# Summing the fourth channel chunk of a 31-tap depthwise convolution on TensorE with diagonal matrices

## The reference, cut to what matters

```python
a_val, a_gate = z[..., :CONV_CH], z[..., CONV_CH:o0]
q = z[..., o0:o0 + ATT_WIDTH]
...
a = a_val * jax.nn.sigmoid(a_gate)
a = dwconv_centred(a, conv_dw, conv_dw_b)      # 31 taps, each channel by itself
a = layernorm(a, conv_ln_g, conv_ln_b)         # over the 512 channels
a = jax.nn.silu(a)
...
q = apply_axial_rope(rmsnorm(q, q_norm_g), tabs)
k = apply_axial_rope(rmsnorm(k, k_norm_g), tabs)
att = gqa_blocked(q, k, v)
mixed = jnp.concatenate([a, att], axis=-1)
return jnp.einsum("bsc,cd->bsd", mixed, w_out)
```

## Time and profile before

| what | value |
|---|---|
| median of 3 runs | 1738.52 us (1733.63 to 1740.14) |
| the profiled execution | 1735.93 us, its span 1734.2 us |
| mean granted clock of PE | 0.962 |
| PE busy | 1545.3 us, 89% of the span |
| DVE busy | 852.6 us, 49% |
| POOL busy | 852.3 us, 49% |
| ACT busy | 399.3 us, 23% |

### The profile page before, as it was taken

The page is one execution under the profiler, slowest core; times in us unless marked ns, Lnnn a source line. Parts: engine busy times, 40 slices in busy tenths (PEclk is TensorE's granted clock), DMA queues, the critical chain, the costliest instruction groups (busy, mean ns, idle before and its releaser), DMA issues.

```text
span 1734.2 us, 18986 instructions
## 1 busy us (share of the span) xinstructions
PE 1545.3 (89%) x7152; PEld 1225.9 (71%) x7152; DVE 852.6 (49%) x1153; ACT 399.3 (23%) x792; POOL 852.3 (49%) x314
## 2 busy tenths in 40 slices
PE   1698999999699999999599588896996999999996
PEld 1676777668588888888587465476765888888884
DVE  4767257543631111211619799534225566656657
ACT  0301123321510101001422233333225211111112
POOL 0365444345346555555258387352434455555661
PEclk9999999999799999999799899998997999999998
DMA  9465321212222223322222121021212122222221
GB/s 325 153 242 182 134 85 49 73 49 98 73 64 95 97 98 97 97 97 87 91 96 73 49 73 49 25 73 61 73 48 74 50 97 97 97 97 88 85 93 49
DMA packets 91555, 161.84 MB, mean 93 GB/s; under 512 B 3381, under 2 KB 44257, under 8 KB 91489
## 3 DMA queue, kind: packets, MB, share of 16 engines
q1 hardware_dynamic: 88000, 153.10, 26.1%
q10 hardware_dynamic: 3489, 7.82, 1.3%
HBM read 158.82 MB, written 2.10 MB: 93 GB/s over the span
## 4 chain that ended last, share of the span: by engine, by line
PE 74%; DVE 16%; ACT 3%; DMA 2%; POOL 2%; issue 2%; ACTq 0%; DVEq 0%; POOLq 0%; SPq 0%
PE bank L569 22%; PE bank L571 22%; PE bank L570 22%; DVE bank L1331 3%; DVE bank L1327 2%; DMA ada_w<-in_w_ada 2%; POOL w_lo L508 2%; DVE ada_acc L1331 2%; DVE smx L1621 1%; DVE x L1327 1%; PE bank L759 1%; DVE p2b L1336 1%; PE bank L887 1%; PE bank L738 1%; ACT xn L1033 1%
## 5 line engine op out<-in xcount | busy, mean ns | idle before, releaser
L506 POOL TENSOR_SCALAR w_hi<-w_raw 128x2048 fp32r<-128x2048 f32 x120 | 230.4, 1920 | 833.8 <-PE bank L569 715.6
L508 POOL TENSOR_TENSOR w_lo<-w_raw,w_hi 128x2048 fp32r<-128x2048 f32 x120 | 555.3, 4627 | 10.0
L569 PE MATMUL bank<-ht_hi,w_hi 128*128 128x512 f32 (+1 forms) x1232 | 456.8, 371 | 12.7 <-POOL w_lo L508 12.2
L570 PE MATMUL bank<-ht_hi,w_lo 128*128 128x512 f32 (+1 forms) x1232 | 454.0, 369 | 0.0
L571 PE MATMUL bank<-ht_lo,w_hi 128*128 128x512 f32 (+1 forms) x1232 | 453.6, 368 | 0.0
L569 PEld LDWEIGHTS bank<-ht_hi,w_hi 128*128 128x128 f32 x1232 | 235.5, 191 | 57.1 <-POOL w_lo L508 12.1
L571 PEld LDWEIGHTS bank<-ht_lo,w_hi 128*128 128x128 f32 x1232 | 235.0, 191 | 41.7
L570 PEld LDWEIGHTS bank<-ht_hi,w_lo 128*128 128x128 f32 x1232 | 235.2, 191 | 41.0 <-issue 0.2
L1327 DVE TENSOR_TENSOR facc<-bank,facc 128x512 f32<-128x512 f32 x104 | 72.0, 692 | 119.4 <-PE bank L571 111.1
L1331 DVE SCALAR_TENSOR_TENSOR uc<-bank,par,uc 128x511 f32<-128x511 f32 x88 | 66.0, 750 | 127.9 <-ACT uc L1299 126.3
L687 PE MATMUL bank<-ident,xn 128*128 128x128 f32 x176 | 36.3, 376 | 75.3 <-ACT xn L1033 75.3
(11 more groups left out here) (214 smaller groups left out, 2252.7 us busy)
## 6 DMA issues: line engine op xcount, KB each, us to landing
w_raw<-in_w_in SPq DMA_DIRECT2D x27, 1024.0 KB, 5.2
ada_w<-in_w_ada SPq DMA_DIRECT2D x48, 512.0 KB, 6.0
w_raw<-in_w_up SPq DMA_DIRECT2D x22, 1024.0 KB, 5.1
w_raw<-in_w_mlp_in SPq DMA_DIRECT2D x16, 1024.0 KB, 5.2
w_raw<-in_w_mlp_out SPq DMA_DIRECT2D x16, 1024.0 KB, 5.1
w_raw<-in_w_down SPq DMA_DIRECT2D x11, 1024.0 KB, 4.9
w_raw<-in_w_out SPq DMA_DIRECT2D x8, 1024.0 KB, 5.1
w_raw<-in_w_mem_kv SPq DMA_DIRECT2D x8, 1024.0 KB, 5.5
```

The source lines that it names most:

```text
L506: g.tensor_scalar(w_hi[:, r], w_raw[:, r], 1.0, 1.0, ALU.mult, ALU.mult).then_inc(slab_hi, 1)
L508: g.tensor_tensor(w_lo[:, r], w_raw[:, r], w_hi[:, r].bitcast(F32), ALU.subtract).then_inc(slab_split, 1)
L569: inc_free(pe.matmul(o, ah, bh, start=start, stop=False))
L570: pe.matmul(o, al, bh, start=False, stop=False)
```

## The change

The fourth chunk is taken from POOL and summed by PE. For each tap POOL makes a diagonal matrix, `tap_m[:, k]` = identity times the channel's tap, 31 in all, in groups of 8, 8, 8 and 7 ahead of the splits of the first four slabs of `w_in_2`. PE multiplies each with the shifted input and adds all of them up in one PSUM tile ("conv"): taps 0 to 8 in the rotary stage behind v's turning, which moves ahead of `kd`, and taps 9 to 30 between z0 and z1. ACT reads the tile, adds the bias and writes `ay[:, 3]`. `kx` goes (its room and more is taken by `tap_m`); what it held is written to `qsq[:, 1]`. The compiler's room for DMA descriptors is set to 1024.

```diff
-POOL_CC = 1
-POOL_TAPS = (2, 2, 3, 1, 2, 3, 3, 3, 3)
+PE_CC = 1
+PE_TAPS = ((0, 9), (9, K2))
+TAP_GROUPS = (8, 8, 8, 7)
...
+    if _step == ("z", 0):
+        ATT2_ORDER.append(("conv", 1))
...
 ROPE_ORDER = [("k", 0), ("ss", 0), ("rot", 0), ("rot", 1), ("v", 0), ("ss", 1), ("rot", 2), ("rot", 3), ("m", 0), ("kss", 0),
-              ("rot", 4), ("m", 1), ("kd", 0), ("kd", 1), ("vt", 0)]
...
+              ("rot", 4), ("m", 1), ("vt", 0), ("conv", 0), ("kd", 0), ("kd", 1)]
...
-            kx = sb("kx", [P, T], where=lend)
             v_t = sb("v_t", [P, T], where=lend)
+            tap_m = sb("tap_m", [P, K2, P], where=lend)
...
-            taps = conv31()
-            n = S0["w_in2"] + 6
+            n = S0["w_in2"]
             split_all(0, n)
-            for k in POOL_TAPS:
-                for _ in range(k):
-                    next(taps, None)
+            k = 0
+            for taps in TAP_GROUPS:
+                for _ in range(taps):
+                    w = V_CDW + CC * k + CC - 1
+                    g.tensor_scalar(tap_m[:, k], ident[:], vec[:, w:w + 1], 1.0, ALU.mult, ALU.mult).then_inc(taps_made, 1)
+                    k += 1
                 split(n)
                 n += 1
-            for _ in taps:
-                pass
...
             split_all(n, NSLAB)
...
+            def conv_taps(part):
+
+                t = Tile(TR["conv", 0])
+                k0, k1_ = PE_TAPS[part]
+                if part == 0:
+                    t.wait_free(pe)
+                    pe.wait_ge(taps_made, K2)
+                    Tile(T0["w_in2a"] + 4 + CC - 1).wait_taken(pe)
+                for k in range(k0, k1_):
+                    ins = pe.matmul(t.ap[:], tap_m[:, k], av[:, CC - 1, k:k + T], start=k == 0, stop=k == K2 - 1)
+                if part:
+                    ins.then_inc(t.full, 1)
...
-            pe.wait_ge(ay_pool_ready, POOL_CC)
+            Tile(TR["conv", 0]).wait_taken(pe)
...
+            copy_out(TR["vt", 0], v2[:].rearrange("p m d -> p (m d)"))
             for g in range(KV2):
                 copy_out(TR["kd", g], k2[:, g])
-            copy_out(TR["vt", 0], v2[:].rearrange("p m d -> p (m d)"))
...
+                    elif what == "conv":
+                        t = Tile(TR["conv", 0])
+                        t.wait_full(act)
+                        st.done(act.activation(ay[:, CC - 1], t.ap[:], ACT.Identity,
+                                               bias=vec[:, V_CB + CC - 1:V_CB + CC]), tile=t)
...
-    nc = bacc.Bacc("TRN2", target_bir_lowering=False, num_devices=1)
+    nc = bacc.Bacc("TRN2", target_bir_lowering=False, num_devices=1, dynamic_dma_scratch_size=1024)
```

More of the change, by code:

```diff
@@ L63 @@
          ("pattn", 8), ("w_out", 8), ("nt2", 8), ("mlp", 16 * FF1_Q), ("nt3", 8), ("w_in2a", 8), ("memnt", 4),
-         ("conv31", CC - POOL_CC), ("q2", CC), ("rope", 1 + 1 + 2 + CC + 1 + 1 + 2 * 2 + 2 + 1), ("att2", 2 * 6 + 9 * H1),
+         ("conv31", CC - PE_CC), ("q2", CC), ("rope", 1 + 1 + 2 + CC + 1 + 1 + 2 * 2 + 2 + 1 + 1), ("att2", 2 * 6 + 9 * H1),
          ("ln", 2), ("w_out2", 8), ("nt4", 8), ("mem_q", 8),
@@ L184 @@
 ROPE_ORDER = [("k", 0), ("ss", 0), ("rot", 0), ("rot", 1), ("v", 0), ("ss", 1), ("rot", 2), ("rot", 3), ("m", 0), ("kss", 0),
-              ("rot", 4), ("m", 1), ("kd", 0), ("kd", 1), ("vt", 0)]
-TR = head_tiles(TILE0["rope"], ROPE_ORDER, {"k": 1, "v": 1, "ss": 1, "rot": 1, "kss": 1, "m": 2, "kd": 1, "vt": 1})
-TT2 = head_tiles(TILE0["att2"], ATT2_ORDER, {"z": NT, "t": NT, "o": 1, "m": 2})
+              ("rot", 4), ("m", 1), ("vt", 0), ("conv", 0), ("kd", 0), ("kd", 1)]
+TR = head_tiles(TILE0["rope"], ROPE_ORDER, {"k": 1, "v": 1, "ss": 1, "rot": 1, "kss": 1, "m": 2, "kd": 1, "vt": 1, "conv": 1})
+TT2 = head_tiles(TILE0["att2"], ATT2_ORDER, {"z": NT, "t": NT, "o": 1, "m": 2, "conv": 0})
 TTM = head_tiles(TILE0["attm"], ATTM_ORDER, {"z": NT, "t": MT, "o": 2})
@@ L333, in build @@
             "tables_made", "q_squared", "rope_std", "ln_std"))
-        ay_pool_ready = sem("ay_pool_ready")
+        taps_made = sem("taps_made")
         ln_d, ln_sq, ln_used, ln_y = (sem(n) for n in ("ln_d", "ln_sq", "ln_used", "ln_y"))
@@ L515, in split_all @@
                     split(b - 1)
[L517 to L535, removed]
-            taps = conv31()
-            n = S0["w_in2"] + 6
-            split_all(0, n)
-            for k in POOL_TAPS:
-                for _ in range(k):
-                    next(taps, None)
+            n = S0["w_in2"]
+            split_all(0, n)
+            k = 0
[4 more added lines that the diff above has]
+                    k += 1
                 split(n)
                 n += 1
-            for _ in taps:
-                pass
+            assert k == K2
             split_all(n, NSLAB)
@@ L828, in k_twice @@
                 Tile(TR["rot", CC]).wait_taken(pe)
-                pe.matmul(t.ap[:], rope_m[:, 2 + g], kx[:], start=True, stop=True).then_inc(t.full, 1)
+                pe.matmul(t.ap[:], rope_m[:, 2 + g], qsq[:, 1], start=True, stop=True).then_inc(t.full, 1)
             def turn_v():
@@ L858, in _ @@
                     turn_v()
+                elif what == "conv":
+                    conv_taps(j)
                 else:
@@ L894, in _ @@
                     all_taken(TR[what, g] for what, g in (("kd", 0), ("kd", 1), ("vt", 0)))
-                {"z": scores2, "t": turn2, "o": values2, "m": memory_kv}[what](h)
+                {"z": scores2, "t": turn2, "o": values2, "m": memory_kv, "conv": conv_taps}[what](h)
             t = Tile(T0["ln"])
             t.wait_free(pe)
-            all_taken(T0["conv31"] + c for c in range(CC - POOL_CC))
-            pe.wait_ge(ay_pool_ready, POOL_CC)
+            all_taken(T0["conv31"] + c for c in range(CC - PE_CC))
+            Tile(TR["conv", 0]).wait_taken(pe)
             for c in range(CC):
@@ L1568, in conv31 @@
             def conv31():
-                for c in range(CC - POOL_CC):
+                for c in range(CC - PE_CC):
                     t = Tile(T0["conv31"] + c)
@@ L1592, in _ @@
                 rot = Tile(TR["rot", c])
-                part, table = (q2[:, c], rope_gq[:]) if c < CC else (kx[:], rope[:, 0])
+                part, table = (q2[:, c], rope_gq[:]) if c < CC else (qsq[:, 1], rope[:, 0])
                 Tile(T0["q2"] + c if c < CC else TR["k", 0]).wait_taken(v)
@@ L1609, in _ @@
                     tt(part, rot.ap[:], tmp[:, 0], ALU.mult, tile=rot)
-            per_tile = -(-((CC - POOL_CC) * K2 - sum(TAPS_BEFORE_ROPE)) // (H1 * NT))
+            per_tile = -(-((CC - PE_CC) * K2 - sum(TAPS_BEFORE_ROPE)) // (H1 * NT))
             def softmax_attention(order, tiles, heads, keys, p_of, minus_scale, mb, ob, out_of, fill):
```

## The result

| kernel | median of its runs | lowest to highest |
|---|---|---|
| before | 1738.05 us (6 runs) | 1733.63 to 1740.47 |
| changed | 1747.8 us (6 runs) | 1744.06 to 1749.02 |

The ratio is 1.0054, with a 95% interval of 1.0038 to 1.0070: the change makes the kernel about half a per cent slower, by 9.75 us between the medians. The forecast was 1748.5 us.

What follows compares the result with a forecast made beforehand. DVE was taken to set the time of a head from 977 us on. 8.15 + 1.0 + 0.5 + 0.4 = +10 us on the median 1738.52 gave 1748.5 us; likeliest case 1743 to 1756, range leaving out 2 in 10 1739 to 1757.

Steps and rivals of the forecast that it cites:

- The tap's price: On PE, each tap is two matmul instructions of 0.4375 us; 62 instructions, 27.1 us for 31 taps.
- two rivals that put it at 0.23 and at 0.6 us: PE's taps at 0.23 us an instruction, 1738 us, chance 0.04; or at 0.6 us, 1758 us, chance 0.09.
- rival 5: The taps on PE wait for POOL's matrices, so the change doesn't do what it says; chance under 0.01.
- Removal worth nothing: Taking the fourth chunk's products and sums, 64.6 us busy, off POOL gains 0 us on the path.
- Matrices under cover: POOL's 31 matrices, 0.4 us each ahead of the first four w_in_2 splits, cost 0 us; fourth split ends at 894.2.
- The first scores: Head 0's scores on PE start near 974.6 instead of 976.17 us, after a faster doubling of k: 1.55 us gained.
- The step: DVE gets head 1's first score tile at 999.5 instead of 991.33 us, behind 22 taps on PE: +8.15 us.
- What came later: Slab splits on POOL hold DVE's scalings longer: +1.0 us in head 1, +0.5 in head 2, +0.4 in head 6.
- Sum: Whole change, DVE's delay at head 1 plus three later terms: 8.15 + 1.0 + 0.5 + 0.4 = +10 us.
- Rival 1: DVE's stall at head 1 is smaller or given back in later heads: +3 to +8 us, 1744 us; chance 0.25.
- Rival 2: Faster: POOL's taps held DVE, or splits fall into DVE's maxima; if all long scalings went, -9.5 us, 1729; chance 0.05.

Runs made afterwards that it cites:

- halved kernel: The changed kernel with 11 taps instead of 22 between z0 and z1, taps 20 to 30 left out: 1736.81 us, ratio to before 0.9998.

## Why the prediction came out right

**The tap's price.** Forecast 0.4375 us an instruction, measured 27.0 / 62 = 0.436. The two rivals that put it at 0.23 and at 0.6 us fall, and so does rival 5: PE's first tap shows no idle time ahead of it.

**Removal worth nothing.** The changed kernel still has long scalings in heads 1 to 6, and they hold DVE 23.6 us above 0.49 each, against 17.6. The halved kernel says the same: where the taps fit, heads 0 to 6 take 121.5 us together, against 121.3 before. (The prediction counts one product twice: the 25.9 us of the earlier trace rows are 30 products, and the first product is the 31st. Nothing hangs on it.)

**Matrices under cover.** Forecast 0.4 us each, measured 0.374. The fourth slab's split follows its seven matrices like this, and ends at 895.3 (forecast 894.2); PE's products don't wait for it (its one wait for a w_lo from 884 to 920 us, 1.3 us at the third slab, is in the kernel before as well).

```profile
886.29 2.46 POOL L526 TENSOR_SCALAR tap_m<-ident,vec 128x128 f32<-128x128 f32 x7
888.73 1.91 POOL L509 TENSOR_SCALAR w_hi<-w_raw 128x2048 fp32r<-128x2048 f32 x1
```

**The first scores.** Forecast 1.55 us earlier, measured 0.25 us earlier by the clock of the trace and 1.78 us against the first product of q. The doubling took 1.88 us for the 1.8 forecast; the run with v alone turned first shows that the clock made most of it, as the prediction's step has it.

**The step.** Forecast +8.15 us at DVE's first tile of head 1, measured 23.57 - 14.03 - 1.78 = +7.76. The wait was 9.65 us where 8 to 9 were forecast. Here the prediction was at odds with its own working: DVE comes to the tile earlier by what the first scores gain, so the wait is the step and that gain, 8.15 + 1.55 = 9.7 us by its own terms. ACT's copy took 0.69 us for 0.78.

**What came later.** Forecast 1.0 (head 1) + 0.5 (head 2) + 0.4 (head 6) = +1.9, measured 0.50 + 1.25 + 0.86, and 0.2 in head 4: +2.8. The mechanism in head 1 is the one forecast, two scalings held. From the timelines of DVE and of POOL:

```profile
1006.58 0.98 DVE L1339 TENSOR_SCALAR p2b<-p2b,smx 128x512 f32<-128x512 f32 x1
...
1009.45 2.84 DVE L1339 TENSOR_SCALAR p2b<-p2b,smx 128x512 f32<-128x512 f32 x1
```

```profile
1005.37 1.91 POOL L509 TENSOR_SCALAR w_hi<-w_raw 128x2048 fp32r<-128x2048 f32 x1 [39.07 <-PE bank L552]
1007.36 4.64 POOL L511 TENSOR_TENSOR w_lo<-w_raw,w_hi 128x2048 fp32r<-128x2048 f32 x1
```

w_hi came 4.75 us into DVE's block where the prediction had it at 5.1, so it holds the scaling 0.49 us and not 1.05. In heads 2 and 6 the scalings are held 4.22 and 4.37 us against 2.36 and 0.90; of the rise, 0.7 and 2.7 us lay in waits that DVE had there before. The run with v turned first shows that such terms turn on a tenth of a microsecond, so their sum being near is partly luck: the -2 to +4 us that the range gave them is the honest figure.

**Sum.** 7.76 + 2.8 = 10.6 us of stage for the 10 us forecast, and 9.75 us between the medians. Rival 1 (stall given back) falls: one of the things that spoke for it did come, as DVE's waits over the heads are gone but for the first tiles of heads 0 and 1 (4.5 and 9.6 us), as this list from 977 to 1110 us shows; but longer holds took their place, and all of the stall is still there at the layer norm.

```profile
DVE smx L1624 <- PE bank L867: 14.1, 2, 9.6
DVE smx L1624 <- DVE smx L1341: 0.5, 1, 0.5
```

```profile
1131.82 3.70 PE L900 MATMUL bank<-ay,ones 128*128 128x512 f32 x8
```

Rival 2 (faster) falls too, since the long scalings stayed with w_lo. Its price was real, though: without the lock the stage is 4.05 us shorter in one form and 6.8 us in the other.

## What to carry to other kernels

A hole on one engine has the length of the block that its partner is working through, so compare new work with that length, piece by piece: eleven taps between two heads' scores were free, 22 cost 10 us, and the same 22 one step later in the order cost 1.6 us. Before moving work off an engine, ask whether anybody waits for it: here all but one of POOL's splits in the heads began after idle time, so the taps held nothing up. And when an engine that sets the pace has instructions of one shape with two very different lengths, look for what runs beside the long ones: taking those away was the only edit here that made the kernel faster. Then compare the traces stage by stage too: a level time or a gain can hold something that the edit wasn't meant to do, as the 2.7 us behind the layer norm did here.

## What was not expected of the hardware

- DVE's scaling and POOL's w_lo split decide their order at 0.02 to 0.08 us, and the scaling that comes second waits for the rest of the split: 4.36 us in the one case, 2.35 us in the other.
- The scaling with an accumulated output was never held in 32 instructions (745 to 750 ns), beside the same splits that hold the plain form until it takes 4.50 us; slower each time by 0.34 us, it still made the kernel 5.5 us faster.
- Filling PE's hole with taps shortened the doubling behind it from 3.64 to 1.88 us for the same four instructions: work that was put in front of them gave back 1.5 us.
- The same last product with the values took 5.31 us before and 3.62 us in two other kernels, in a stretch at a granted clock of 0.87 and of 1.00: 1.7 us that no edit aimed at.
